# Barriers taken out between the state-space stage and the second output projection, and filler tiles moved, in a three-layer mixer kernel

## The reference

```python
x = first_block(...)          # RWKV heads, pooling, stick-breaking attention
x = even_layer(...)           # chunked attention and a state-space model
x = odd_layer(...)            # forgetting attention
return rmsnorm(x, final_norm_g)
```

```python
yb = _pool(pu, pool_w[l], pool_scale[l]) * jax.nn.silu(pg)      # first layer

q, k, v, u, z_a, z_b = jnp.split(proj, cuts, axis=-1)           # second layer
o_a = chunked_relpos_attention(q, k, v, rel_bias)
o_a = o_a * jax.nn.silu(z_a)
y = jax.nn.gelu(s5_ssm(u, ...))
o_b = y * jax.nn.sigmoid(y @ w_glu + b_glu)
o_b = o_b * jax.nn.silu(z_b)
return x + jnp.concatenate([o_a, o_b], axis=-1) @ w_out
```

## Time and profile before

| | us |
|---|---|
| median of 3 runs | 3088.73 |
| lowest and highest of them | 3087.23, 3088.84 |
| the profiled execution, its own time | 3082.84 |
| its span in the trace | 3081.0 |
| TensorE busy (18138 matmuls) | 2961.1 |
| VectorE, ScalarE, GpSimd busy | 1187.9, 1184.4, 1194.9 |

### The profile page before, as it was taken

One profiled execution on the slowest core, in us unless ns is written; L12 is line 12 of the kernel. 1 busy time (PEld: TensorE's weight loads), 2 busy tenths in 40 slices (PEclk: granted clock), 3 DMA queues, 4 the chain that ended last, 5 costly groups with the idle time before them and its releaser, 6 DMA issues.

```text
span 3081.0 us, 46589 instructions
## 1 busy us (share of the span) xinstructions
PE 2961.1 (96%) x18138; PEld 2357.0 (76%) x18138; DVE 1187.9 (39%) x1719; ACT 1184.4 (38%) x1600; POOL 1194.9 (39%) x546
## 2 busy tenths in 40 slices
PE   7999999989998998999989989999999999999997
PEld 6777777767876887777767767887888888888786
DVE  6555555343443128777713434114111111111112
ACT  5433334255655223333334543324333332333322
POOL 1222222423235435666533323434433333333542
PEclk9999999999999999999999999999999999999998
DMA  5221111322122533322332323543332332333243
GB/s 204 63 57 57 57 57 56 100 65 75 61 83 89 150 120 103 94 90 95 99 120 83 96 79 103 160 123 97 86 95 88 86 94 86 94 88 92 87 125 108
DMA packets 92290, 290.12 MB, mean 94 GB/s; under 512 B 10240, under 2 KB 12416, under 8 KB 91152
## 3 DMA queue, kind: packets, MB, share of 16 engines
q1 hardware_dynamic: 67392, 242.45, 26.3%
q10 hardware_dynamic: 24784, 46.02, 4.5%
HBM read 269.52 MB, written 18.91 MB: 94 GB/s over the span
## 4 chain that ended last, share of the span: by engine, by line
PE 73%; DVE 12%; issue 9%; POOL 3%; ACT 1%; DMA 1%; DVEq 0%; PEld 0%; ACTq 0%; PEldq 0%; POOLq 0%; SPq 0%
PE ps L343 14%; PE ps L345 14%; PE ps L344 14%; PE ps L911 4%; PE ps L913 4%; PE ps L912 4%; PE ps L1218 2%; POOL w_lo L2713 2%; PE ps L1220 2%; PE ps L1219 2%; DVE arena L2618 1%; PE ps L1283 1%; DVE arena L2588 1%; PE ps L1760 1%; PE ps L1778 1%
## 5 line engine op out<-in xcount | busy, mean ns | idle before, releaser
L2713 POOL TENSOR_TENSOR w_lo<-raw,w_hi 128x1024 fp32r<-128x1024 f32 x436 | 1059.3, 2432 | 1824.3 <-ACT w_hi L651 1822.6
L343 PE MATMUL ps<-act_hi,w_hi 128*128 128x512 f32 x2208 | 877.3, 397 | 23.8 <-DVE act_lo L616 9.5
L345 PE MATMUL ps<-act_lo,w_hi 128*128 128x512 f32 x2208 | 863.6, 391 | 0.0
L344 PE MATMUL ps<-act_hi,w_lo 128*128 128x512 f32 x2208 | 863.3, 391 | 0.0
L651 ACT ACTIVATE w_hi<-raw 128x1024 fp32r<-128x1024 f32 x440 | 464.0, 1055 | 619.0 <-PE ps L345 344.5
L343 PEld LDWEIGHTS ps<-act_hi,w_hi 128*128 128x128 f32 x2208 | 416.5, 189 | 127.4 <-issue 20.8
L344 PEld LDWEIGHTS ps<-act_hi,w_lo 128*128 128x128 f32 x2208 | 417.1, 189 | 87.9 <-issue 4.1
L345 PEld LDWEIGHTS ps<-act_lo,w_hi 128*128 128x128 f32 x2208 | 416.9, 189 | 88.0
L911 PE MATMUL ps<-act_hi,w_hi 128*128 128x512 f32 x736 | 295.0, 401 | 2.0 <-ACT arena L999 2.0
L912 PE MATMUL ps<-act_hi,w_lo 128*128 128x512 f32 x736 | 287.4, 391 | 0.0
L913 PE MATMUL ps<-act_lo,w_hi 128*128 128x512 f32 x736 | 287.2, 390 | 0.0
(11 more groups left out here) (411 smaller groups left out, 3524.2 us busy)
## 6 DMA issues: line engine op xcount, KB each, us to landing
raw<-stream SPq DMA_DIRECT2D x440, 512.0 KB, 3.6
residual<-mix ACTq DMA_DIRECT2D x32, 256.0 KB, 2.1
arena<-residual ACTq DMA_DIRECT2D x32, 256.0 KB, 2.7
arena<-x_rows SPq DMA_DIRECT2D x4, 1024.0 KB, 18.7
arena<-x ACTq DMA_DIRECT2D x16, 256.0 KB, 2.8
kept_qk<-mix ACTq DMA_DIRECT2D x16, 256.0 KB, 2.0
arena<-kept_qk ACTq DMA_DIRECT2D x16, 256.0 KB, 4.0
arena<-decays ACTq DMA_DIRECT2D x16, 256.0 KB, 3.1
```

The lines of the kernel that those rows point to most:

```text
L343: pe.matmul(dst, w_hi[:, slot, j, :], act_hi[:, kt, :], start=first, stop=False)
L344: pe.matmul(dst, w_lo[:, slot, j, :], act_hi[:, kt, :], start=False, stop=False)
L345: mm = pe.matmul(dst, w_hi[:, slot, j, :], act_lo[:, kt, :], start=False, stop=last)
L2713: nc.gpsimd.tensor_tensor(w_lo[:, s, :, :], raw[:, s % 2, :, :], w_hi[:, s, :, :].bitcast(F32), ALU.subtract).then_inc(split_done, 1)
```

## The change

1. Pooling: the filler tiles are dealt out one to each of the first three pooling matmuls and two to the last; one more follows the last. TensorE no longer waits at barrier 2, it only counts itself in.
2. Barriers 5, 6 and 7 are gone. In place of number 5, TensorE waits for the last state-space output (`s5_out`).
3. The two weight tiles behind the state-space stage move into `even_tensor`, and the first `turn` goes between the two halves of the second. The load of q and k for unit 0 is issued in the last state-space tile, the biases ahead of the four weight rounds.
4. The roundings of `mix` 8 to 15 for the gated stage move from unit 7 to the end of unit 6. Gated tile 0 runs behind the scores of unit 7, gated tile 1 behind its transposes.
5. The gates are loaded in four pieces, into slots that are free already in unit 7. Sigmoids and products of gated tile 0 (and the sigmoids of tile 1) are computed inside unit 7, where `mix` 0 to 6 are rounded for the projection too.
6. The projection's tiles are turned by eight places: `mix` tile t is held at place (t + 8) % 16 of `act_hi` and `act_lo`, so that the attention tiles come first and don't overwrite the inputs of the gated stage; the weight blocks are still taken in stream order.

```diff
-        def gemm(pe, n, par, free=None, act_ready=None, halves=(0, 1), outputs=1):
+        def gemm(pe, n, par, free=None, act_ready=None, halves=(0, 1), outputs=1, turned=0):
...
-                bank = h if outputs == 2 else par
+                bank = (N_GLU + h) % 2 if outputs == 2 else par
...
-                    pe.matmul(dst, w_hi[:, slot, j, :], act_hi[:, kt, :], start=first, stop=False)
+                    a = (kt + turned) % KT
+                    pe.matmul(dst, w_hi[:, slot, j, :], act_hi[:, a, :], start=first, stop=False)
...
-            if between is None and k0 == 0:
-                pe.wait_ge(split_done, n * 2 + 4)
...
+                if j == 0:
+                    pe.wait_ge(split_done, n * 2 + h + 3)
...
+        TURNED = (0, HK, 0)
...
-        def mix_split_scalar(act, layer):
...
-        def mix_split_vector(dve, layer):
...
+        def turned_round(act, tiles):
+
+            for ft in tiles:
+                nc.scalar.activation(act_hi[:, (ft + HK) % KT, :], mix_tile(ft), ACT.Copy).then_inc(mix_hi, 1)
+
+        def turned_rest(dve, tiles):
+
+            for ft in tiles:
+                dve.wait_ge(mix_hi, KT + ft + 1)
+                nc.vector.tensor_tensor(act_lo[:, (ft + HK) % KT, :], mix_tile(ft),
+                                        act_hi[:, (ft + HK) % KT, :].bitcast(F32), ALU.subtract).then_inc(mix_lo, 1)
...
         def pool_tensor(pe):
+            def tile(i):
+                n = N_POOL + i
+                gemm(pe, n, n % 2, free=(evac_act, n - 1))
+
             for g in range(POOL_GROUPS):
-
-                if g < POOL_GROUPS - 1:
-                    for n in range(N_POOL + 2 * g + 4, N_POOL + 2 * g + 6):
-                        gemm(pe, n, n % 2, free=(evac_act, n - 1))
+                tile(g + 4)
+                if g == POOL_GROUPS - 1:
+                    tile(g + 5)
...
+            arrive(pe)
+            tile(POOL_GROUPS + 5)
...
                 half(0, 0)
                 half(0, 1)
+                if not more:
+                    gemm(pe, N_GLU, N_GLU % 2, free=(evac_act, GLU_TAKEN - 1), act_ready=(glu_lo, 0), outputs=2)
...
                 if not more:
-                    pe.wait_ge(evac_act, GLU_TAKEN)
-                    gemm(pe, N_GLU, N_GLU % 2, outputs=2, act_ready=(glu_lo, 0))
+                    gemm(pe, N_GLU + 1, (N_GLU + 1) % 2, free=(evac_act, GLU_TAKEN + 1), outputs=2)
...
+            first, second = N_EVEN, N_EVEN + 1
+            gemm(pe, first, first % 2, free=(evac_act, first - 17))
+            gemm(pe, second, second % 2, free=(evac_act, second - 17), halves=(0,))
             turn(0)
+            gemm(pe, second, second % 2, halves=(1,))
+            pe.wait_ge(s5_out, S5_TILES)
...
-                    act.wait_ge(pe_half, 2 * N_GLU)
-                    for i in range(8):
-                        nc.scalar.activation(act_hi[:, i, :], mix_tile(8 + i), ACT.Copy).then_inc(glu_hi, 1)
+                    load_gates(act, GATES_LATE, gates_late)
+                    glu_sigmoids(act, 0)
...
+                    if isinstance(u, int) and u == EV_PAIRS - 2:
+                        act.wait_ge(pe_half, 2 * N_GLU - 1)
+                        for i in range(HK):
+                            nc.scalar.activation(act_hi[:, i, :], mix_tile(8 + i), ACT.Copy).then_inc(glu_hi, 1)
...
+                else:
+                    turned_round(act, range(EV_PAIRS - 1))
+                    glu_sigmoids(act, 1)
+                    V.wait(act, "mix", u)
+                    turned_round(act, (EV_PAIRS - 1,))
...
+            ahead(0)
+            ahead(1)
+            take(0, 0)
+            ahead(2)
+            values(0)
+            take(0, 1)
+            ahead(3)
...
+                    glu_products(dve, (0, 1))
+                    turned_rest(dve, range(EV_PAIRS - 1))
...
+        def glu_scalar(act):
+            glu_sigmoids(act, 2)
+            glu_sigmoids(act, 3)
+            for ft in range(EV_PAIRS, KT):
+                act.wait_ge(glu_mul, ft - EV_PAIRS + 1)
+                turned_round(act, (ft,))
...
+        def glu_vector(dve):
+            turned_rest(dve, (EV_PAIRS - 1,))
+            for o in range(2, 8):
+                glu_products(dve, (o,))
+            turned_rest(dve, range(EV_PAIRS, KT))
...
             sb_tensor(pe)
...
-            meet(pe, 5)
             even_tensor(pe)
-            meet(pe, 6)
             glu_tensor(pe)
-            meet(pe, 7)
             out_tensor(pe, 1, N_OUT2, GLU_TAKEN + 8)
```

More of the change, by code:

```diff
@@ L368, in gemm_two @@
                         b.then_inc(pe_half, 1)
-                if between is not None:
-                    between(kt)
         sq = [slots(arena, 24), slots(arena, 25)]
@@ L480, in out_tensor @@
                 for j in range(2):
-                    gemm(pe, ft + (n0 + j), (n0 + j) % 2, free=(evac_dve, ft + (KT * layer + j - 1)))
+                    gemm(pe, ft + (n0 + j), (n0 + j) % 2, free=(evac_dve, ft + (KT * layer + j - 1)), turned=turned)
             if layer == 2:
@@ L2049, in values, with ahead @@
                 nc.scalar.activation(ev_v, ps[:, 7, :], ACT.Copy).then_inc(ev_copied, 1)
+            def ahead(i):
+                cast(act, N_EVEN * 2 + 4 + i, (2 * N_EVEN + i) % 4)
+            ahead(0)
[5 more added lines that the diff above has]
+            ahead(3)
             for par in range(2):
                 act.wait_ge(spilled[par], 16 * 12)
-            load_qk(0, 0)
-            take(0, 0)
-            values(0)
-            take(0, 1)
             unit(0, 0, True)
@@ L2106, in unit @@
                 V.finish()
+                if isinstance(u, int) and u == EV_PAIRS - 2:
+                    for j in range(HK):
+                        dve.wait_ge(glu_hi, j + 1)
+                        nc.vector.tensor_tensor(act_lo[:, j, :], mix_tile(8 + j), act_hi[:, j, :].bitcast(F32),
+                                                ALU.subtract).then_inc(glu_lo, 1)
             unit(0)
@@ L2298, in s5_tensor @@
             tile(S5_TILES - 1, 1, False)
-            for n in (N_EVEN, N_EVEN + 1):
-                gemm(pe, n, n % 2, free=(evac_act, n - 17))
         def s5_scalar(act):
@@ L2381, in tile @@
                     gelu(i - 1)
+                if not more:
+                    A.wait(act, "cos", i)
+                    load_qk(act, 0, 0)
                 spill(i, 1, 1 - par)
@@ L2741, in _ @@
             pool_tensor(pe)
-            meet(pe, 2)
             sb_tensor(pe)
```

113 lines of the change are left out of this document (49 added, 64 removed).

## The result

| | before | changed |
|---|---|---|
| median us, first session (4 and 4 runs) | 3087.98 | 3040.35 |
| lowest and highest | 3085.36, 3088.84 | 3039.15, 3042.32 |
| ratio, 95% interval | | 0.9849 (0.9837 to 0.9861) |
| median us, second session (7 and 4 runs) | 3087.05 | 3045.03 |
| lowest and highest | 3083.9, 3089.12 | 3042.05, 3046.79 |

The change makes the kernel 47.6 us faster in one session and 42.0 us in another. The forecast was 3042 us, within 3036 to 3056. The profiled execution of the first session took 3042.32 us, with a span of 3040.4.

A forecast was written before the change was run, and what follows sets the result against it. TensorE, busy 96% of the span, bounds the kernel; gains lie only in its waits and lower clock. Gains 9.3 + 13.3 + 24.2 = 46.8 us take 3082.84 to 3036.0; a 5.9 us offset gives 3042, range 3036 to 3056.

The forecast's parts named there:

- the last average: Pooling: TensorE waited for VectorE's last average, 7.98 us after the third pooling matmul; two weight tiles (21.6 us) should cover it.
- one tile covers the third: Pooling: the third average takes 9.5 us, under the 10.8 us of one weight tile, with 1.3 us to spare.
- The gap at the end: End of pooling: from tile end through ScalarE's weight round and barrier back to TensorE, priced at 2.7 us.
- a pooling matmul: Pooling: each of the two pooling matmuls in the new closing stretch was priced at 0.5 us.
- ScalarE arrives, TensorE goes on: End of pooling: TensorE goes on instead of both engines meeting; 0.3 us was put down for the barrier.
- The terms hold: State space to attention: transposes 0.5, scores 2.4, changes of matmul kind 0.4, so 3.3 against 16.6 us; gain 13.3.
- The cover: Before the projection: seven attention tiles rounded by about 1835, the other eight behind the last sigmoid; without it, at most 8 us.
- the median lies 5.9 us higher, and the same offset gives 3041.9: Sum: the timed median before lay 5.9 us above the profiled execution; the same offset lifts 3036.0 to 3041.9.
- A: New wait at one place: VectorE held by GpSimd splits (first mechanism) or biases delaying weights (second); 3045 to 3056, chance 0.27.
- B: Gated stage: its chain takes over, TensorE waits at each gated tile, last part gives 14.6 us less; 3057, chance 0.06.
- C: Whole kernel slower: low clock granted in unbroken work and staying; 3104 with twelve weight tiles at it, chance 0.02.
- D: Nothing changes: the barriers are replaced by data waits of equal length; 3089, chance 0.01.

The follow-up runs named there:

- E1: Changed kernel with its pooling part undone (two filler tiles behind each of the first three pooling matmuls, TensorE waiting at barrier 2); 3050.98 us.
- E5: Changed kernel with barriers 6 and 7, around the gated stage, put back on all three engines; 3052.83 us.
- E10: Changed kernel with one filler tile between each pair of pooling matmuls and two behind the last; 3045.58 us.
- E6: Changed kernel with its pooling order kept, but TensorE waiting at barrier 2 again behind its last pooling tile; 3040.48 us.
- E2: Changed kernel with the end of the state-space stage as before: filler tiles there, barrier 5 behind them, then biases, then q and k; 3056.26 us.
- E8: Changed kernel with q and k of unit 0 issued behind the biases and value transposes behind the second weight tile, barrier still gone; 3041.4 us.
- E3: Changed kernel with both pooling and the end of the state-space stage as before, last attention unit and gated stage as changed; 3064.47 us.
- E7: Changed kernel with gated tile 0 moved back behind the transposes of the last attention unit; 3052.14 us.
- E9: Changed kernel with mix 0 to 7 rounded and split behind the last sigmoid of the gated stage, same turned order, no barrier; 3049.05 us.
- R1: The changed kernel itself, without an edit, profiled and timed a second time; 3045.03 us.
- R2: The kernel before the change, profiled a second time; 3087.79 us.
- E4: Changed kernel with 12 of 18 opening matmuls of the first output projection moved ahead of the first triangular group, last stick-breaking unit; 3038.32 us.

## Why the prediction was right

**Pooling: 9.3 predicted, 8.8 in the trace, 8.8 in E1's median and 8.9 in its trace.** The step that named the cause, the last average, holds, and so does the claim that one tile covers the third: 7.5 us against 9.5 reckoned. The 9.5 held two blocks of VectorE by GpSimd's splits (2.25 us each, at 594.77 and 597.64 in the trace of before); in the new order there is one. The gap at the end is 2.30 us (2.7 reckoned). What was sized too low is a pooling matmul, 0.5 us: from one to the next (569.59 to 581.37) it is 11.8 us with a tile of 10.8 between, so about 1.0. That the gap keeps the full clock was true of the first profile and not of the second, where 622 to 626 reads 0.58, nor of E5's and E10's; there the stretch from the first average to the sums of squares is 1.4 to 1.5 us longer. Charging nothing for it was luck of the execution. The step "ScalarE arrives, TensorE goes on" was costed as 0.3 us; E6 shows nothing to be had there.

**State space to attention: 13.3 predicted, 13.7 in the trace, 14.1 in E2.** The terms hold. The prediction did not separate which move earns it. E8 narrows it down: not the order of q, k and biases, and hardly the place of the transposes (0.78 us), but the early issue of the transfers, with the barrier gone and the weight rounds behind the biases. Which of these two was needed wasn't tried.

**Last unit to projection: 24.2 predicted, 23.8 in the trace, 23.2 in E3.** The terms held: 10.8 for a tile, 2.34 for the transposes, 0.78 at the last sigmoid. E7 prices the filled wait at 9.9 us, the wait and the clock; E5 the two barriers at 10.6. The 4.47 us that the prediction called a wait at a barrier were more than that: with the barrier back but the sigmoids of gated tile 0 early, E5 waits 1.49 us there. The cover came on time to the microsecond: seven tiles rounded by about 1835 was reckoned on the clock of the kernel before, and 1815.4 with the 19.2 us of lead is 1834.6. Its price "if that cover were gone" was at most 8 us; with only the attention tiles late, E9 measured 4.0, half of the longer wait from the held subtraction.

**Sum: 46.8 predicted, 46.3 at the three places.** In the two sessions the medians give 47.6 and 42.0. One step was weak though it did no harm: "the median lies 5.9 us higher, and the same offset gives 3041.9". The profiled execution of before was at the low end of its runs (11 others of one session took 3083.08 to 3089.42), while the two of the changed kernel were the slowest of theirs. The offset is no property of the program; 46.8 from the median of 3088.73 gives the same number without it.

**Rivals.** A did not happen at the changed places. Its first mechanism exists (a copy of 2.25 us in each of three averages, a subtraction of 2.80 us in E9), but strikes once an average and inside the cover; its second shows as a weight round 0.4 us late, hidden. That round and the 8.9 us of the biases are also the rows that bear on transfers of two queues side by side; q and k and the biases of the earlier trace rows all came from ScalarE's queue. B, C and D find nothing in the traces: no gated tile waits, the 72 us read 1.00, and the waits are gone.

The 2.4 us that the pair of first profiles lost behind 1868, and the 2.5 us in the pair R1 and R2 (43.69 us ahead at the third projection tile, 41.2 at the end), aren't the change's either. From the third projection tile to the end, before and R2 take 1169.7 us, the changed kernel's two profiles 1172.0 and 1172.2; but E1, E2, E3, E4, E6 and E10, whose code there is that of the changed kernel, take 1169.3 to 1169.6, and the other four 1170.6 to 1173.5. The clock differs with it: from 2830 to 2870, for instance, it reads 0.91 and 0.93 in the two profiles of the changed kernel, and 1.00 in E4, E6 and E10 (and from 2870 to 2910 in both of before). What stays open is what decides in which execution the clock falls there.

## What to carry to other kernels

Price a barrier by what stands between TensorE's last need and the arrival of the slowest engine: here it was nothing for one barrier and 10 to 12 us for two others. Ask too what a barrier, and the program order around it, keeps from being issued early: with the transfers issued 21 us before their use, the wait of 6.96 us for q and k was gone, though which of the two had held them wasn't separated. A filler tile goes where the longest chain is, and one tile (11 us) for each chain of 8 us is enough; the second bought nothing (E10). Compare a change of 1% by its stretches in the trace as well as by its median, since the same program moves by several microseconds between executions and sessions.

## What the runs showed of the hardware

**The low clock moves from execution to execution, and waits answer it.** The spans of one program go with its mean granted clock: the kernel before took 3081.3 and 3081.9 us at 0.985 and 0.986, and 3087.6 at 0.983; the changed one 3037.0 at 0.992, and 3040.4 and 3044.8 at 0.989. A wait of 2.30 us before L914 was followed by 1.00 in one execution of the changed kernel and by 0.58 in the other:

```profile
620.00:624.00 4.00, 4.00 (x15) 2.61 (x15) 0.47 (x1) 3.08 (x5) 0.10 (x1) 1.00 0.41 131
```

```profile
622.00:626.00 4.00, 4.00 (x10) 2.82 (x9) 0.00 (x0) 1.90 (x3) 0.03 (x1) 0.58 0.38 131
```

So a short wait can cost one time and not the next. And where the clock falls early, TensorE comes later to the next wait and waits less: the stretch from 932 to 939 reads 0.53 in E8 and 0.79 in the changed kernel's first profile, TensorE comes to the wait of the last stick-breaking unit 11.3 us behind the opening matmul of the pair in E8 and 9.8 us in the other, and in both the wait ends 14.4 us behind that matmul. It is 3.14 us long in one and 4.65 in the other. The Trainium skill, TensorE: Matmul & The Clock Gate, Part 1, says that the gate's observation runs freely and doesn't restart with a kernel, so that the point of transition varies; the executions of one program above agree.

**VectorE can be held by GpSimd for the rest of a split, however small its own instruction**: a copy of 128x2 took 2.25 us, and a 128x512 subtraction 2.80 us, beside splits of 2.96 and 2.72 us. Not every instruction is: in the changed kernel's first profile a 128x512 `TENSOR_TENSOR` with one input in `ps` ran from 68.08 to 68.76 inside a split from 67.86 to 70.25, as thirty such did in 0.68 to 0.69 us each, and one on a single column (128x1) took 0.16 us inside the next split.
